# The second up projection on the un-normed residual, with the shift as pad columns and the root put on the products

## The reference, cut to what matters

```
lat = lat + g1 * yl
hl  = modulate(rmsnorm(lat, norm_g[l, 1]), sh2, sc2)
lat = lat + g2 * conv_ffn(hl, ffn_w_up, ffn_conv_w, ffn_conv_b, ffn_w_down)

rmsnorm(x, g)      = x * rsqrt(mean(x*x) + EPS) * g
modulate(h, sh, sc) = h * (1 + sc) + sh
conv_ffn(h): u = dwconv(h @ w_up, conv_w, conv_b)     # 3 taps over positions, zero padded
             gate, val = split(u, 2)
             return (silu(gate) * val) @ w_down
```

## Time and profile before

| what | value |
|---|---|
| median of the runs | 872.11 us |
| the profiled execution, its own time | 871.97 us |
| its span | 870.2 us |
| TensorE busy | 859.8 us |
| ScalarE busy | 488.6 us |
| weight loads of TensorE, busy | 768.5 us |
| mean rate of all transfers | 185 GB/s |

### The profile page before, as it was taken

The page is one execution under the profiler, slowest core; times in us unless marked ns, Lnnn a source line. Parts: engine busy times, 40 slices in busy tenths (PEclk is TensorE's granted clock), DMA queues, the critical chain, the costliest instruction groups (busy, mean ns, idle before and its releaser), DMA issues.

```text
span 870.2 us, 16530 instructions
## 1 busy us (share of the span) xinstructions
PE 859.8 (99%) x6054; PEld 768.5 (88%) x6054; DVE 657.1 (76%) x1118; ACT 488.6 (56%) x774; POOL 0.2 (0%) x4
## 2 busy tenths in 40 slices
PE   8999999999999999999999999999999999999997
PEld 3688888888899999999998899999998888888886
DVE  4793899999997788877668797766577767666665
ACT  5433677777765654555557545555545555444444
POOL 0000000000000000000000000000000000000000
PEclk9999999999999999999999999999999999999999
DMA  9974444444446657556564554444465456555551
GB/s 346 408 290 154 148 144 147 145 145 145 165 153 237 193 201 249 177 199 192 170 196 142 199 189 147 152 164 147 145 218 168 128 192 214 193 193 183 181 191 49
DMA packets 45441, 160.90 MB, mean 185 GB/s; under 512 B 5200, under 2 KB 6608, under 8 KB 45264
## 3 DMA queue, kind: packets, MB, share of 16 engines
q1 hardware_dynamic: 43488, 156.43, 52.7%
q10 hardware_dynamic: 1904, 3.81, 1.2%
HBM read 159.16 MB, written 1.05 MB: 184 GB/s over the span
## 4 chain that ended last, share of the span: by engine, by line
PE 93%; DVE 3%; ACT 2%; DMA 1%; issue 1%; SPq 1%; DVEq 0%; ACTq 0%
PE bank L418 19%; PE bank L420 18%; PE bank L419 18%; PE bank L439 6%; PE bank L483 5%; PE bank L485 5%; PE bank L484 5%; PE bank L440 3%; PE bank L1232 2%; PE bank L1236 2%; PE bank L1240 2%; DMA arena<-in_ada 1%; PE bank L451 1%; PE bank L1358 1%; PE bank L1201 1%
## 5 line engine op out<-in xcount | busy, mean ns | idle before, releaser
L412 DVE TENSOR_TENSOR w_lo<-raw,w_hi 128x1024 fp32r<-128x1024 f32 x244 | 295.1, 1223 | 100.9 <-ACT w_hi L405 100.7
L405 ACT ACTIVATE w_hi<-raw 128x1024 fp32r<-128x1024 f32 x244 | 252.7, 1051 | 92.2 <-PE bank L420 45.1
L418 PE MATMUL bank<-h_both,w_hi 128*128 128x256 f32 (+1 forms) x928 | 281.2, 303 | 0.0
L419 PE MATMUL bank<-h_both,w_hi 128*128 128x256 f32 (+1 forms) x928 | 276.2, 298 | 0.0
L420 PE MATMUL bank<-h_both,w_lo 128*128 128x256 f32 (+1 forms) x928 | 275.9, 297 | 0.0
L418 PEld LDWEIGHTS bank<-h_both,w_hi 128*128 128x128 f32 x928 | 174.4, 188 | 8.2 <-issue 1.3
L420 PEld LDWEIGHTS bank<-h_both,w_lo 128*128 128x128 f32 x928 | 175.0, 189 | 5.7
L419 PEld LDWEIGHTS bank<-h_both,w_hi 128*128 128x128 f32 x928 | 174.8, 188 | 5.2
L418 PE MATMUL bank<-y_hi,w_hi 128*128 128x256 f32 x304 | 87.0, 286 | 0.1
L419 PE MATMUL bank<-y_lo,w_hi 128*128 128x256 f32 x304 | 85.6, 281 | 0.0
L420 PE MATMUL bank<-y_hi,w_lo 128*128 128x256 f32 x304 | 85.5, 281 | 0.0
(11 more groups left out here) (283 smaller groups left out, 1194.9 us busy)
## 6 DMA issues: line engine op xcount, KB each, us to landing
raw<-in_stream SPq DMA_DIRECT2D x244, 512.0 KB, 3.4
arena<-in_ada SPq DMA_DIRECT2D x40, 512.0 KB, 7.2
xres<-in_ada SPq DMA_DIRECT2D x8, 512.0 KB, 3.3
tok<-in_tok SPq DMA_DIRECT2D x4, 512.0 KB, 5.4
con<-in_con ACTq DMA_DIRECT2D x1, 1472.0 KB, 6.2
xres<-in_tok ACTq DMA_DIRECT2D x1, 1024.0 KB, 8.4
out<-arena SPq DMA_DIRECT2D x4, 256.0 KB, 2.0
arena<-in_post_mix ACTq DMA_DIRECT2D x1, 512.0 KB, 4.1
```

The lines of the kernel that those rows point to most:

```text
L405: act.activation(w_hi[c.slot][:, :], raw[c.slot][:, :], ACT.Copy).then_inc(S("split_hi"), 1)
L412: dve.tensor_tensor(w_lo[c.slot][:, :], raw[c.slot][:, :], w_hi[c.slot][:, :].bitcast(F32), ALU.subtract).then_inc(S("split_lo"), 1)
L418: pe.matmul(dst, hi_w, a_hi, start=start, stop=False, skip_group_check=True)
L419: pe.matmul(dst, hi_w, a_lo, start=False, stop=False, skip_group_check=True)
```

## The change

The input of the up projection is now lat * (1 + sc2) * g, without root and shift (`scaled_hi`, `scaled_lo`, which were there for the next block and now take the gain and the place). It has 258 columns a tile (FW): the 256 tokens and one pad column at either end, and both pad columns hold the negated shift. Each up product is 258 wide. VectorE multiplies it by the root, with 1.0 at the pad columns (`ffn_scaled`), and puts it into SBUF (`z_f`). In the pad columns it then holds -(sh2 @ w_up). The missing shift goes into the bias of the middle tap: ScalarE forms it with one small operation for each half, as pad column times `conv_sum` (the negated sum of the three taps' weights) plus the old bias. The left and right taps are read from `z_f` at full width; at the edge they meet the pad column, so that the shift drops out there.

The matmul of the first up tiles therefore comes before squares and root. The first four up tiles are reordered (value 0, gate 1, gate 0, value 1); the first two run as the tiles of the residual come. The squares are added by VectorE (`add_squares`, seven additions), one matmul with ones sums them in the middle of the fourth up tile (`squares_sum`). `norm_sum`, `pair_squares`, `split_h_hi` and `norm_input` are gone, and so are the eight unread matmuls here. VectorE's list in the stage has its splits between the steps of a tile. The gate sums move from VectorE to GpSimd, as a multiplication and an addition for each row, and SyncE loads rows 4 to 7 with one group of stream chunks between two of them.

```diff
-        def norm_sum(pe, bank=7):
-        def pair_squares(dve):
+        def add_squares(dve):
+            for n, (to, by) in enumerate(((0, 1), (2, 3), (4, 5), (6, 7), (0, 2), (4, 6), (0, 4))):
...
+                dve.tensor_tensor(x, x, wide[:, by * T:by * T + T], ALU.add).then_inc(S("squares_added"), 1)
+        def squares_sum(pe, bank):
+            pe.wait_ge(S("squares_added"), QUARTERS + KT - 1)
+            pe.matmul(psum[bank][:, 0:T], ones, wide[:, 0:T], start=True, stop=True).then_inc(S("norm_summed"), 1)
...
 sync:
-                    sp.wait_ge(S("gate_summed"), k - 3)
+                    sp.wait_ge(S("gate_summed"), 2 * (k - 4) + 1)
-            for u in range(1, 5):
+            for u in range(1, 7):
                 load_stream(i_ffn + u)
-                for k in (2 * u - 2, 2 * u - 1) if u >= 3 else ():
-                    load_gate(k)
+                if u >= 3:
+                    load_gate(u + 1)
...
 scalar:
+            act.activation(shift_columns(h_hi), shifts, ACT.Copy, scale=-1.0).then_inc(S("mod_rows"), 1)
...
             hi(act, Chunk(N_FFN, 1))
+            hi(act, Chunk(N_FFN, 2))
+            for m in range(KT):
+                scaled_hi(act, 0, m, gain_2, padded_at)
+            hi(act, Chunk(N_FFN, 3))
             square_residual(act, 0)
-            hi(act, Chunk(N_FFN, AHEAD))
-            norm_rstd(act, 0, 1)
-            split_h_hi(act, 1, lambda m: mod[:, 3 * KT + m:3 * KT + m + 1])
+            hi(act, Chunk(N_FFN, 4))
+            hi(act, Chunk(N_FFN, 5))
+            norm_rstd(act, 0, 1, bank=3, dst=rstd[:, 1:1 + T])
...
+            def ffn_middle(t, p, has_old):
+                    act.activation(z_bias[p][:, half:half + 1], z_f[p][half][:, 0:1], ACT.Identity,
+                                   scale=conv_sum[:, bass.ds(t + half * JF, 1)], bias=p1("conv_b", t + half * JF)).then_inc(S("z_bias"), 1)
...
+                    act.activation(conv[p][half], z_f[p][half][:, 1:1 + T], ACT.Identity,
...
 tensor:
-            norm_sum(pe)
-            keep_clock(pe, HOUT_BANKS[0], IDLE)
+            first_columns_late(pe, [Chunk(N_FFN), Chunk(N_FFN, 1)], [psum[6][:, 0:FW], psum[5][:, 0:FW]], 2 * KT, width=FW)
+            pe.wait_ge(S("residual"), KT)
+            column_tile(pe, Chunk(N_FFN, 2), psum[4][:, 0:FW], FW, FW)
+            column_tile(pe, Chunk(N_FFN, 3), psum[7][:, 0:FW], FW, FW, lambda: squares_sum(pe, 3), KT // 2)
+            def ffn_up(j, p, c):
+                pe.wait_ge(S("z"), j * 2 - 2)
+                column_tile(pe, c[0], psum[4 + p][:, 0:FW], FW, FW)
+                column_tile(pe, c[1], psum[6 + p][:, 0:FW], FW, FW)
...
+        @block.gpsimd
+            for k in range(KT):
+                pool.wait_ge(S(f"mod_loaded{k % 4}"), 16 * (k // 4 + 3))
...
+                    pool.tensor_scalar(x, x, c_k, None, ALU.mult).then_inc(S("gate_summed"), 1)
+                    pool.wait_ge(S("gate_summed"), 2 * k)
+                    pool.tensor_tensor(gate_sum, x, gate_sum, ALU.add).then_inc(S("gate_summed"), 1)
...
 vector:
             add_product(dve, lambda m: mod[:, 2 * KT + m:2 * KT + m + 1], 0, N_FFN, HOUT_BANKS)
-            pair_squares(dve)
-            lo(dve, Chunk(N_FFN, AHEAD))
+            for m in range(KT):
+                scaled_lo(dve, 1, m, gain_2, padded_at)
+            for k in range(2, 6):
+                lo(dve, Chunk(N_FFN, k))
+                if k == 3:
+                    add_squares(dve)
+            dve.memset(rstd[:, 0:FW:FW - 1], 1.0).then_inc(S("final_weights"), 1)
             dve.wait_ge(S("norm_rstd"), 2 * 1)
-            norm_input(dve, 1, lambda m: gain_2[:, m:m + 1], lambda m: mod[:, 3 * KT + m:3 * KT + m + 1])
...
+            def ffn_scaled(t, p, n_done):
+                dve.wait_ge(S("multiplied"), n_done)
+                for half in range(2):
+                    dve.tensor_tensor(z_f[p][half], psum[4 + 2 * half + p][:, 0:FW], padded_rstd, ALU.mult).then_inc(S("z"), 1)
...
             for j in range(1, FFN_PEEL):
+                ffn_scaled(t, p, N_FFN + 3 if t == 0 else ffn_first(t) + 2)
                 if j >= 2:
                     lo(dve, Chunk(c, AHEAD))
+                ffn_taps(t, p)
+                if j >= 2:
+                    lo(dve, Chunk(c, 1 + AHEAD))
+                ffn_gated(t, p)
                 if j >= 2:
                     lo(dve, Chunk(c, 2 + AHEAD))
+                ffn_lo(t, p, s)
```

More of the change, by code:

```diff
@@ L122 @@
 COL = 32
-GATE_ROWS = (0, 0, 1, 1, 1, 1, 1, 1, 1, 1)
+FW = T + 2
 PIECES = (0, 2, 4, 6, 8)
@@ L269, in build @@
         x_weight = tiny(2)
+        conv_sum = tiny(2 * JF)
+        z_bias = [tiny(2) for _ in range(2)]
         rstd = part(TC)
@@ L306, in build @@
         u_f = [part(T) for _ in range(2)]
+        used[0] = TC + 8 * T
+        z_f = [[part(FW) for _ in range(2)] for _ in range(2)]
+        used[0] = TC + 8 * T
         m_low = [part(T) for _ in range(2)]
@@ L450, in first_columns_late @@
                     for w in (w_hi, w_lo):
-                        pe.matmul(dst, w[c.slot][:, k * P:k * P + P], h_hi[:, k * T:k * T + T], start=k == 0 and w is w_hi,
+                        pe.matmul(dst, w[c.slot][:, k * P:k * P + P], h_hi[:, k * width:(k + 1) * width], start=k == 0 and w is w_hi,
                                   stop=False, skip_group_check=True)
@@ L507, in over_tiles @@
             return x.rearrange("p (o t) -> p o t", o=1).broadcast_to([P, n, x.shape[1]])
-        def norm_sum(pe, bank=7):
-            for m in (0, 1, 2, 3, 4, 6):
-                if m < 4:
-                    pe.wait_ge(S("norm_squares"), m + 1)
-                else:
-                    pe.wait_ge(S("plain"), m // 2 - 1)
-                last = pe.matmul(psum[bank][:, 0:T], ones, wide[:, m * T:m * T + T], start=m == 0, stop=m == 6)
-            last.then_inc(S("norm_summed"), 1)
-        def pair_squares(dve):
[L522 to L525, removed]
+        def add_squares(dve):
+            for n, (to, by) in enumerate(((0, 1), (2, 3), (4, 5), (6, 7), (0, 2), (4, 6), (0, 4))):
+                if n < 4:
+                    dve.wait_ge(S("norm_squares"), by + 1)
+                else:
+                    dve.wait_ge(S("squares_added"), QUARTERS + (2, 4, 6)[n - 4])
+                x = wide[:, to * T:to * T + T]
+                dve.tensor_tensor(x, x, wide[:, by * T:by * T + T], ALU.add).then_inc(S("squares_added"), 1)
+        def squares_sum(pe, bank):
+            pe.wait_ge(S("squares_added"), QUARTERS + KT - 1)
+            pe.matmul(psum[bank][:, 0:T], ones, wide[:, 0:T], start=True, stop=True).then_inc(S("norm_summed"), 1)
         def keep_clock(pe, bank, n):
@@ L587, in scale_residual, with plain_at @@
             dve.scalar_tensor_tensor(x, x, p1("final", m), final_rstd, ALU.mult, ALU.mult).then_inc(S("residual"), 1)
[L591 to L598, removed]
+        def plain_at(m):
+            return slice(m * T, m * T + T)
@@ L599, in scaled_hi, with padded_at, scaled_lo @@
+        def padded_at(m):
+            return slice(m * FW + 1, m * FW + 1 + T)
+        def scaled_hi(act, update, m, gain, at):
             wait_residual(act, update, m)
-            act.activation(h_hi[:, x], xres[:, x], ACT.Copy, scale=final_pre[:, m:m + 1]).then_inc(S("h_hi"), 1)
-        def scaled_lo(dve, q, m):
-            x = slice(m * T, m * T + T)
+            act.activation(h_hi[:, at(m)], xres[:, m * T:m * T + T], ACT.Copy, scale=gain[:, m:m + 1]).then_inc(S("h_hi"), 1)
+        def scaled_lo(dve, q, m, gain, at):
@@ L604, in scaled_lo @@
             dve.wait_ge(S("h_hi"), (q + 1) * KT + m + 1)
[L605 to L616, removed]
+            dve.scalar_tensor_tensor(h_lo[:, at(m)], xres[:, m * T:m * T + T], gain[:, m:m + 1], h_hi[:, at(m)].bitcast(F32),
+                                     ALU.mult, ALU.subtract).then_inc(S("h_lo"), 1)
@@ L1777, in _ @@
                 x = wide[:, k * TC:(k + 1) * TC]
-                dve.tensor_tensor(x, x, wide[:, (k + 1) * TC:(k + 2) * TC], ALU.add).then_inc(S("tok_added"), 1)
+                dve.tensor_tensor(x, x, wide[:, (k + 1) * TC:(k + 2) * TC], ALU.add).then_inc(S("squares_added"), 1)
             dve.wait_ge(S("tok_rstd"), 4)
@@ L2022, in _ @@
             lo(dve, Chunk(N_HOUT, 7))
+            dve.wait_ge(S("mod_rows"), QUARTERS + 3)
+            dve.scalar_tensor_tensor(shift_columns(h_lo), shifts, -1.0, shift_columns(h_hi).bitcast(F32), ALU.mult, ALU.subtract).then_inc(S("final_weights"), 1)
             out_gated(HEADS - 1, 1)
```

146 lines of the change are left out of this document (78 added, 68 removed).

## The result

The changed kernel takes 877.88 us (median of 4 runs, 877.34 to 878.88) against 872.11 (4 runs, 872.04 to 872.23): a ratio of 1.0068, 95% interval 1.0056 to 1.0081. Its profiled execution has a span of 875.7 us, 5.5 more than before. I had forecast 869.2. The forecast was wrong in its sign; the time is the one that rival 1 gave for GpSimd operations twice as long as VectorE's, 877.6.

The account below looks back on a forecast made before the run. TensorE, busy for 99% of the span, was taken to bound the kernel. Terms of -5.40 + 0.95 + 0.43 + 0.8 + 0.3 = -2.9 us took 872.1 to 869.2 us; own range 868.1 to 870.3, wider range 868.2 to 878.5.

Parts of the forecast that it names:

- rival 1: Transition, from about 272.5 us: GpSimd's gate operations hold VectorE up; 872.2 to 874.4, 877.6 or up to 885 us; light 17%, heavy 30%.
- part 5: Gate sums moved to GpSimd: VectorE loses 9.7 us that TensorE's work hid, nothing gained, own cost 0.
- a cover of 0.1 us only: Chunk 50's split on VectorE ends at 277.4, TensorE wants it at 277.5; any longer delay goes into the time.
- the forecast without exclusion: Whole kernel, GpSimd not holding VectorE up: 869.2 us, with its neighbours up to 870.3; 46%.
- the heavy case: Transition: rival 1 with GpSimd holding VectorE up strongly, 874 to 885 us; 30%.
- Part 1: Gap between last output projection and first up projection matmul goes, first up matmul about 271.7; 5.40 us removed.
- Part 2: Up projection: 1,056 matmuls of 258 columns instead of 256, priced by a straight line to 512; cost 0.95 us.
- Rival 2: Up projection: a matmul of 258 columns has a step in its time; ending at 871.4 or 872.4 us; 5%.
- Part 3: Fourth up tile: one matmul sums the squares, 0.43 us, with no wait and 1.2 us to spare.
- Part 4: New waits: 0.8 us before the third up pair, 0.3 before the first down projection; the loop stays TensorE's.
- The sum: Whole kernel: -5.40 + 0.95 + 0.43 + 0.8 + 0.3 = -2.9 us, giving 869.2 us.

Follow-up runs that it names:

- e4: The changed kernel with each of GpSimd's 15 operations replaced by a fill of 128x1024, the gate sum left out; 868.9 us.
- e10: The changed kernel with GpSimd's eight multiplications replaced by fills, the seven additions kept, the gate sum left out; 877.24 us.
- e8: The changed kernel with GpSimd's seven additions replaced by fills, the eight multiplications kept, the gate sum left out; 870.18 us.
- e1: The changed kernel with the gate sums back on VectorE, one row behind each pair of tiles from the third on (the last gets two); 872.27 us.
- e2: The changed kernel with GpSimd's gate sums begun only when two feed-forward tiles are done, loads of rows 4 to 7 later; 876.67 us.
- e9: e1 with ScalarE rounding a pair's third chunk ahead of the product's high part and the squares' sum three weight tiles earlier; 868.41 us.
- e11: The kernel of e2 with e9's two edits of order; 870.06 us.
- e7: The kernel before with the gate sums on GpSimd, begun only when two feed-forward tiles are done; 872.05 us.
- e3: The kernel before with only the gate sums moved to GpSimd, at the transition, loads spread as in the change; 881.27 us.

## Why the prediction was wrong, step by step

**The step that failed is in part 5: "Own cost 0; the other end is the first rival".** What it put at nothing without a row was GpSimd's hold on VectorE at the transition, and the runs show about 9 us for it: 877.88 after against 868.9 with fills (e4). I had GpSimd's and VectorE's lists at the right place, 272 us, with "a cover of 0.1 us only", and named the mechanism and a price of 877.6. Then I gave the forecast without exclusion 46% and the heavy case 30%, because no row of the kernel before shows GpSimd computing. That was the wrong weight. The absence of a row bore out neither case, and the Trainium skill's rule ("SBUF — State Buffer", "Who interferes with whom") was a definite statement for this pair of operations. The traces agree with its core: fills, which read nothing, cost nothing (e4); VectorE's operations with one SBUF input kept their time beside a multiplication (3.23 us); those with two were held until an addition had ended (2.88 and 2.05 us after, 9.21 in e10). Where it says that the later one always waits for a whole instruction, they agree only in part: two splits and most of the adds of squares ran while the addition of 276.54 was under way, and that one stretched to 6.97 us.

**The size inside the rival** was right by luck, of two errors that cancelled. I took twice VectorE's time for both kinds. The additions are 2.35 to 2.41 us, 1.9 to 2.0 times a split's 1.22, as the Trainium skill, "GPSIMD Engine Reference", section 3, has it. The multiplications are 2.85, 3.8 times VectorE's 0.75. But they hold VectorE much less (e8: 1.3 us), and instead the stage behind the transition lost more. From the first down tile to the column sum it took 169.18 us after, 167.02 in e4.

**Part 1** held: first matmul at 271.70, and 458.35 for the column sum of e4 against my 458.5.

**Part 2** was mis-sized: 0.95 us forecast, nothing measured. e4's stretch holds 912 matmuls of 258 columns and 480 of 256 in 167.02 us, 0.1200 us each, the same as the 0.1200 of 256 columns alone in the earlier trace rows (1,488 in 178.56). The straight line between 256 and 512 columns doesn't hold just above 256. Rival 2 fell with it. (Its "1.07 clocks a column" is a slip: 0.235 us for 512 columns at 2.4 GHz are 1.10, and 0.120 for 256 are 1.13.)

**Part 3** held without GpSimd: no wait for the squares in e4. After, 0.67 us.

**Part 4**: the waits were 0.79 and 0.48 us in e4 (forecast 0.8 and 0.3), and the second is longer because chunk 54's split ended at 291.19 and not 290.65: the root products ended 0.3 us later than I had it, and the chain behind them took 6.4 us in place of 6.15. Its statement on the loop was wrong: "6.7 us against TensorE's 8.7". A round takes VectorE 7.85 (root products at 289.30 and 297.15 in e4). In it VectorE waits 1.43 us in each pair for the high part of the third chunk, which ScalarE rounds only behind the product's high part. I had counted durations and not that hand-over. Without GpSimd or gate rows it doesn't matter: e4's stage has no wait. With either it made e1 and e2 slow. In e9 and e11 ScalarE rounds that chunk earlier, and a round in which VectorE is behind takes it 6.4 us (root products at 322.66 and 329.05 in e11).

**The sum** for the case that I described, no interference, was -2.9 us; e4 has 868.9, 3.25 us less than the 872.15 beside it. Errors of the parts 2 and 4 nearly cancelled: 0.68 us too little up to the first down tile (291.33, forecast 290.65), and 0.83 too much from there to the column sum (167.02, forecast 458.5 - 290.65 = 167.85), where the width's price was nothing.

## What to carry to other kernels

Before work moves to GpSimd, list what VectorE does in the same microseconds: an addition of two SBUF tensors there can hold a VectorE operation with two SBUF inputs until it ends, and what that costs is, in the main, the overlap less VectorE's spare time at that place (0 in e7, 9 us in e3, for the same 15 operations). Look also at the operands that the change gives VectorE: a tap that reads PSUM and one that reads SBUF are not exposed alike. Count spare time from start to start of a whole round in a trace, hand-overs between engines included, and not as a sum of durations. Where a rule of the Trainium skill names exactly the pair of operations that a change puts side by side, the want of a row in the trace before is no evidence against it.

## What the runs showed of the hardware that I had not expected

A multiplication by a scalar on GpSimd (128x1024, one input) takes 2.85 us undisturbed, longer than an addition of two tensors at 2.35 to 2.41, and a fill takes 0.96. A multiplication can be stretched (7.33 us in e8) or hold VectorE a little (eight low parts 0.8 us longer beside one that kept its 2.85). The additions kept their time at e10's transition, but one was stretched to 6.97 us after. What decides which of the two gives way I didn't settle. A wait or an operation with one SBUF input just before it isn't needed for VectorE to be held: e2's right taps at 310.12 followed the left ones without a gap. A matmul of 258 columns costs no more than one of 256, 0.1200 us from start to start (e4, 912 of them among 480 of 256).
